# Hyena's filter inputs loaded first, both filters' taps with places of their own, and the second response behind the first modulation rows

## The chip, the cores and the metric

One core of a Trainium2 chip runs the whole program in one launch. The metric is the time of one execution on the device in microseconds (us), as a median over several runs.

## The reference, cut to what matters

Two transformer blocks (DEPTH = 2) work on a context of 256 tokens and a latent of 256 tokens, width 1024. Every block has a modulated FFN (SwiGLU, hidden width 2816), a mixer, and a second FFN. The first block's mixer holds a Hyena segment. What the change touches are the inputs of these steps:

```python
m_lat = jnp.split(s_lat @ ada_w[l] + ada_b[l], 9, axis=-1)        # modulation, s = silu(c)
h_lat = post_norm_residual(h_lat, swiglu(modulate(h_lat, m_lat[0], m_lat[1]), ...), ...)
...
def hyena_filters(L, w1, b1, f1, w2, b2, f2, w3):
    h = jnp.sin(f1 * (z @ w1 + b1))       # z: (L, 33), constant
    h = jnp.sin(f2 * (h @ w2 + b2))       # (L, 64)
    h = (h @ w3).astype(f32).reshape(L, HY_ORDER, 2, HY_W)         # 2 filters, 2 directions, 512 channels
    return h * window[:, None, None, :]
```

The filters depend on parameters alone. Each filter's two directions are combined and taken to the frequency domain by products with a matrix of cosines and sines. The kernel calls that its response, and it is used only in the Hyena segment, far behind the first FFN.

## The kernel before, in words

The tokens stand feature by feature in eight tiles `h[:, k]` of 128 features and 512 tokens (256 of context, 256 of latent). Products with large weights are made three times in a rounded format: ScalarE copies a piece of weights or a tile of tokens to its rounded value (`hi`, L629, and `u_round`, L666), GpSimd or VectorE forms the remainder (L2033, L1552), and TensorE adds hi*hi, hi*lo and lo*hi. A gate/up pair of the first FFN is 2 times 8 times 3 = 48 such products of 512 columns. Products of full fp32 operands (`mm`, L948) appear in the profile as two passes each.

Every engine has one fixed order of work, and engines wait for each other on semaphores. SP issues the loads of large weights on its queue; ScalarE issues all the others on its own queue before its first computation. The arena in SBUF is one buffer whose ranges are used again by stages that follow one another.

The start of the program, up to the first FFN, is what the change reorders:

- Loads. SP: six blocks of modulation weights (`load_ada`, L458, 1.5 MB each, blocks c = 0 to 5), then, once three of them are used, chunk 0 of the up/gate weights (L467), blocks 6 and 7, and chunk 1. ScalarE's queue (L564): identity, 18 parameter rows, four token tiles of 512 KB, the 12 filter inputs under semaphore `ld_filt` (zT, w1, w2, four columns of hyp with 64 elements each, w3, window, skip, dft, sin0), and four constants. w3, window, dft and sin0 are 1.66 MB together.
- TensorE: parameter rows turned (L953), tokens turned in eight banks of PSUM (L960) and copied by ScalarE (L614); then w1's product, modulation blocks 0 and 1, w2's product, blocks 2 to 4, the taps of filter 0 (`taps_of`), block 5, the response of filter 0 (`response_of`, 10 products of fp32, 20 passes), block 6, the taps of filter 1, block 7, the turn of the modulation rows (`ada_turn`), the response of filter 1, and a wait for its copies.
- VectorE: after w1's and w2's product the argument of the sine in seven steps (L1491 to L1502), then for each filter the window product (L1532), two corrections of one row, difference and sum (L1537, L1539). Both filters use the same SBUF ranges `taps` and `tap_m`, and the same banks of PSUM, so `taps_free` (raised in VectorE's code) holds back filter 1's taps until filter 0's response is computed and copied. `modulation(0)` (L1509 to L1521) follows both filters.
- ScalarE: Silu of c, token copies, two Sin, copies of response 0 (`filter_out`, L640 and L642), copy of the modulation rows (L619), copies of response 1, four weight pieces (`first_pieces`, L629), then for each k the modulated tile and its rounded copy (`u_round(0)`, L661 and L666).
- The first gate/up pair (`first_pair`) needs these tiles one by one. SP waits for both responses (`filt_dft` 2) before it loads the second row of modulation weights and chunk 2 of up/gate.

## Time and profile before

| | |
|---|---|
| median of 3 runs | 2609.51 us (2609.12 to 2609.9) |
| profiled execution, its own time | 2611.09 us |
| its span | 2609.3 us |
| mean granted TensorE clock | 0.921 |
| TensorE busy | 2260.9 us, 87% |
| VectorE, ScalarE, GpSimd busy | 971.6, 743.0, 932.6 us |

The span is the stretch from the first to the last instruction in one profiled execution; the own time is what that execution took on the device. Engines work beside each other, so their shares do not add up. An idle stretch matters only where it lies on the chain of waits that ends last. PE is TensorE, PEld its weight load, DVE VectorE, ACT ScalarE, POOL GpSimd, SPq and ACTq the queues on which SP and ScalarE issue loads.

### The profile page before, as it was taken

How to read it: one execution, taken by the hardware profiler on the slowest of the kernel's cores; microseconds unless marked ns; L12 is line 12 of the kernel's file. 1: busy time of each engine (PE TensorE's matmuls, PEld its weight loads, DVE VectorE, ACT ScalarE, POOL GpSimd, SP SyncE). 2: the span in 40 equal slices, each digit the busy share in tenths (PEclk: the TensorE clock that was granted, in tenths of full speed). 3: DMA queues.
4: the chain of work that ended last, by engine and by line, in shares of the span. 5: the costliest groups of instructions: out<-in, count | busy, mean ns of one | idle time of the engine just before them, and what ended most of it. 6: DMA issues, size and time to landing. Idle time of an engine off the chain costs nothing.

```text
span 2609.3 us, 35528 instructions
## 1 busy us (share of the span) xinstructions
PE 2260.9 (87%) x15423; PEld 1833.2 (70%) x15423; DVE 971.6 (37%) x1412; ACT 743.0 (28%) x1080; POOL 932.6 (36%) x421
## 2 busy tenths in 40 slices
PE   5799999899956687786899999799999898468996
PEld 2477877588435687685677877577888687367996
DVE  2333032522486545545533022532133400635312
ACT  1412121443031111013622122432122354115433
POOL 0244434354042101102443434343444353015884
PEclk8799999899987898888999999899999898658998
DMA  9164354131000000002264354255222130013551
GB/s 329 57 208 143 121 174 153 65 115 55 12 1 2 2 3 2 2 3 97 89 201 145 121 178 154 89 169 194 95 94 87 41 135 33 0 65 107 192 186 65
DMA packets 176091, 259.66 MB, mean 100 GB/s; under 512 B 3925, under 2 KB 146275, under 8 KB 175876
## 3 DMA queue, kind: packets, MB, share of 16 engines
q1 hardware_dynamic: 172192, 250.62, 28.7%
q10 hardware_dynamic: 3748, 6.81, 0.8%
q8 instruction: 121, 1.98, 0.3%
q14 instruction: 30, 0.25, 0.0%
HBM read 256.37 MB, written 1.05 MB: 99 GB/s over the span
## 4 chain that ended last, share of the span: by engine, by line
PE 77%; DVE 14%; ACT 5%; issue 2%; DMA 1%; ACTq 1%; POOL 0%; DVEq 0%; POOLq 0%
PE psum L948 76%; DVE arena L1819 2%; ACT arena L661 2%; ACT u_hi L666 1%; DVE arena L1793 1%; DVE arena L1843 1%; DVE h L1603 1%; DMA arena<-k_sin 1%; ACTq L564 1%; DVE arena L1760 1%; DVE arena L1841 0%; DVE arena L1771 0%; DVE tmp L1616 0%; ACT tmp L711 0%; DVE arena L1737 0%
## 5 line engine op out<-in xcount | busy, mean ns | idle before, releaser
L2033 POOL TENSOR_TENSOR w_lo<-arena,w_hi 128x1024 fp32r<-128x1024 f32 x332 | 813.0, 2454 | 1162.9 <-ACT w_hi L629 1160.4
L948 PE MATMUL psum<-u_hi,w_hi 128*128 128x512 f32 (+1 forms) x1888 | 700.3, 371 | 84.9 <-ACT u_hi L666 49.5
L948 PE MATMUL psum<-u_hi,w_lo 128*128 128x512 f32 (+1 forms) x1888 | 689.1, 365 | 0.0
L948 PE MATMUL psum<-u_lo,w_hi 128*128 128x512 f32 (+1 forms) x1888 | 668.7, 362 | 0.0
L629 ACT ACTIVATE w_hi<-arena 128x1024 fp32r<-128x1024 f32 x332 | 348.4, 1056 | 746.2 <-PE psum L948 734.5
L948 PE MATMUL psum<-arena 64*64 64x64 f32 (+7 forms) x5828 | 440.1, 276 | 104.0 <-DVEq L1799 27.7
L948 PEld LDWEIGHTS psum<-u_hi,w_hi 128*128 128x128 f32 x1888 | 362.7, 192 | 184.4 <-issue 50.1
L948 PEld LDWEIGHTS psum<-arena 64*64 64x64 f32 (+4 forms) x5828 | 356.5, 165 | 181.3 <-issue 70.5
L948 PEld LDWEIGHTS psum<-u_hi,w_lo 128*128 128x128 f32 x1888 | 363.2, 192 | 54.1
L948 PEld LDWEIGHTS psum<-u_lo,w_hi 128*128 128x128 f32 x1888 | 357.5, 190 | 52.8 <-issue 0.2
L1573 DVE TENSOR_TENSOR tmp<-psum,tmp 128x512 f32<-128x512 f32 (+1 forms) x88 | 54.9, 624 | 593.0 <-ACT tmp L685 593.0
L948 PE MATMUL psum<-hid_hi,w_hi 128*128 128x512 f32 (+1 forms) x704 | 257.4, 366 | 1.7 <-POOL w_lo L2033 1.2
L948 PE MATMUL psum<-hid_hi,w_lo 128*128 128x512 f32 (+1 forms) x704 | 255.3, 363 | 0.0
L948 PE MATMUL psum<-hid_lo,w_hi 128*128 128x512 f32 (+1 forms) x704 | 255.2, 363 | 0.0
L1577 DVE TENSOR_TENSOR hid_lo<-tmp,hid_hi 128x512 f32 (+1 forms) x88 | 198.7, 2258 | 10.8
L948 PEld LDWEIGHTS psum<-hid_hi,w_hi 128*128 128x128 f32 x704 | 132.9, 189 | 24.5 <-DVE mods L1509 1.7
L948 PEld LDWEIGHTS psum<-hid_lo,w_hi 128*128 128x128 f32 x704 | 132.9, 189 | 21.1 <-issue 0.7
L948 PEld LDWEIGHTS psum<-hid_hi,w_lo 128*128 128x128 f32 x704 | 132.9, 189 | 20.7
L685 ACT ACTIVATE tmp<-psum 128x512 f32<-128x512 f32 (+1 forms) x88 | 47.9, 544 | 303.3 <-PE psum L948 303.2
L815 ACT ACTIVATE arena<-psum 128x256 f32<-128x256 f32 x96 | 37.1, 386 | 239.3 <-PE psum L948 238.7
L1587 DVE SCALAR_TENSOR_TENSOR h<-psum,mods,h 128x256 f32<-128x256 f32 x56 | 22.3, 475 | 197.3 <-PE psum L948 197.3
L1603 DVE SCALAR_TENSOR_TENSOR h<-psum,mods,h 128x256 f32<-128x256 f32 x80 | 35.2, 478 | 147.9 <-PE psum L948 147.9
(245 smaller groups left out, 1637.9 us busy)
## 6 DMA issues: line engine op xcount, KB each, us to landing
arena<-in_ada_w SPq DMA_DIRECT2D x48, 1536.0 KB, 7.0
arena<-in_ffn_wg SPq DMA_DIRECT2D x44, 1024.0 KB, 5.4
arena<-in_ffn_wu SPq DMA_DIRECT2D x44, 1024.0 KB, 8.0
arena<-in_ffn_wd SPq DMA_DIRECT2D x20, 2048.0 KB, 8.0
arena<-in_ev_w_in SPq DMA_DIRECT2D x6, 2048.0 KB, 7.8
arena<-in_od_w_in SPq DMA_DIRECT2D x6, 2048.0 KB, 8.3
arena<-in_ffn_wd SPq DMA_DIRECT2D x4, 1024.0 KB, 5.0
arena<-in_ev_w_out SPq DMA_DIRECT2D x2, 2048.0 KB, 10.8
```

Of the source, the lines that this page charges most:

```text
L564: act.dma_start(dst, src).then_inc(S(name), 16)
L629: act.activation(piece_shape(split_hi(pc), src), src, ACT.Copy).then_inc(S("hi_done"), 1)
L661: ins = act.activation(us[:, k, s_], hs[:, k, s_], ACT.Identity, scale=modv[:, 24 * (g % 3) + 8 + k, s_:s_ + 1], bias=modv[:, 24 * (g % 3) ...
L666: act.activation(uhv[:, k, T0:NT], uv[:, k, T0:NT], ACT.Copy).then_inc(S("u_hi"), 1)
L685: act.activation(tmp[:, jf * NT:jf * NT + TN], bank[2 * jf][:, 0:TN], ACT.Silu)\
L815: act.activation(blocks(zs[:, d].rearrange("p h t -> p (h t)"), m, d), blocks(bank[d], m, d), ACT.Copy).then_inc(S("zs"), 1)
L948: return pe.matmul(dst, w, x, start=first_, stop=last, skip_group_check=True)
L1573: ve.tensor_tensor(prod, bank[2 * jf + 1][:, 0:TN], prod, ALU.mult).then_inc(S("pairs_free"), 1)
L1577: ve.tensor_tensor(hid_lo[:, at], prod, hid_hi[:, at].bitcast(F32), ALU.subtract)\
L1603: ins = ve.scalar_tensor_tensor(out=hs[:, k, s], in0=bank[b][:, lo:lo + SEG], scalar=modv[:, 24 * (g % 3) + 16 + k, s:s + 1], in1=hs[:, k, s],
L1819: ve.copy_predicated(nm[:, d, 2 * cc + e].rearrange("p (q a) t -> p q (a t)", q=2), mk, bank[n_bank(d, cc, e)].rearrange("p (q t) -> p q t ...
L2033: pool.tensor_tensor(piece_shape(split_lo(pc), src), src, piece_shape(split_hi(pc).bitcast(F32), src), ALU.subtract).then_inc(S("lo_done"), 1)
```

## The change

The seven inputs of the filter's MLP are issued first on SP's queue under a semaphore of their own (`ld_mlp`), modulation block 0 follows, then the five large or late filter inputs (`ld_filt`), then blocks 1 to 5. The MLP's two products stand ahead of and between the parameter rows' and the tokens' turns; the sine's argument is a function that VectorE calls ahead of and behind the parameter copies, and ScalarE's Sin, Silu, Sin stand ahead of the token copies. Tokens are turned in a ring of five banks. The taps of each filter have SBUF ranges of their own, so that only the PSUM banks are waited for (`taps_read`); the two responses use different banks for two of their five results. dft and sin0 lie in a part of the arena that modulation block 0 has not got. TensorE computes the taps of both filters and the first response between the blocks 0 to 3, then blocks 4 to 7 and their turn, then the second response. Its copies on ScalarE follow `u_round(0)`, and the wait for them stands ahead of the second gate/up pair. The first weight pieces stand ahead of the modulation rows' copy.

```diff
@@ -260,6 +260,8 @@
+        TOK_RING = 5
+
@@ -274,8 +276,9 @@
         stage = [big[:, 4096 + i * P:4096 + (i + 1) * P] for i in range(3)]
         w3 = big[0:HY_FO, 4608:6656]
         win = big[:, 6656:7680].rearrange("p (a c) -> p a c", a=2)
-        taps = big[:, 7680:9728].rearrange("p (d a c) -> p d a c", d=2, a=2)
-        tap_m = big[:, 9728:10752].rearrange("p (a c) -> p a c", a=2)
+        taps = [at.rearrange("p (d a c) -> p d a c", d=2, a=2) for at in (big[:, 7680:9728], big[:, 2048:4096])]
+        tap_m = [at.rearrange("p (a c) -> p a c", a=2) for at in (big[:, 9728:10752], big[:, 4608:5632])]
+        FILT_BANK = ((0, 1, 3, 4, 5), (6, 7, 3, 4, 5))
@@ -287,8 +290,8 @@
         kf = arena[:, 40448:45568].rearrange("p (o i c) -> p o i c", o=2, i=5)
-        dft = arena[:, 16384:17408].rearrange("p (a f) -> p a f", a=2)
-        sin0 = arena[:, 18432:18688].rearrange("p (a f) -> p a f", a=2)
+        dft = arena[:, 44544:45568].rearrange("p (a f) -> p a f", a=2)
+        sin0 = arena[:, 43520:43776].rearrange("p (a f) -> p a f", a=2)
@@ -530,7 +533,21 @@
-            for c in range(6):
+            def load_filter(name, dst, src):
+                sp.dma_start(dst, src).then_inc(S(name), 16)
+
+            load_filter("ld_mlp", zT, K["k_zT"])
+            load_filter("ld_mlp", fw1, A["hy_f_w1"][0])
+            for i, name in enumerate(("hy_f_b1", "hy_f_freq1", "hy_f_b2", "hy_f_freq2")):
+                load_filter("ld_mlp", hyp[0:HY_FO, i:i + 1], A[name].rearrange("e n -> n e"))
+            load_filter("ld_mlp", fw2, A["hy_f_w2"][0])
+            load_ada(0, 0)
+            load_filter("ld_filt", w3, A["hy_f_w3"][0])
+            load_filter("ld_filt", big[:, 6656:7680], K["k_win"])
+            load_filter("ld_filt", skip_row, A["hy_skip"].rearrange("e o c -> e o c"))
+            load_filter("ld_filt", arena[:, 44544:45568], K["k_dft"])
+            load_filter("ld_filt", arena[:, 43520:43776], K["k_sin0"])
+            for c in range(1, 6):
                 load_ada(0, c)
             sp.wait_ge(S("ada_used"), 3)
             load_up("up_a", 0, 0, 0)
@@ -590,28 +607,22 @@
             for b in range(4):
                 src = A["ctx"] if b < 2 else A["x"]
                 load("ld_tok", tok_in[:, b, :], src[0, (b % 2) * P:(b % 2 + 1) * P, :])
-            load("ld_filt", zT, K["k_zT"])
-            load("ld_filt", fw1, A["hy_f_w1"][0])
-            load("ld_filt", fw2, A["hy_f_w2"][0])
-            for i, name in enumerate(("hy_f_b1", "hy_f_freq1", "hy_f_b2", "hy_f_freq2")):
-                load("ld_filt", hyp[0:HY_FO, i:i + 1], A[name].rearrange("e n -> n e"))
-            load("ld_filt", w3, A["hy_f_w3"][0])
-            load("ld_filt", big[:, 6656:7680], K["k_win"])
-            load("ld_filt", skip_row, A["hy_skip"].rearrange("e o c -> e o c"))
-            load("ld_filt", arena[:, 16384:17408], K["k_dft"])
-            load("ld_filt", arena[:, 18432:18688], K["k_sin0"])
             load("ld_const", mean_w[:, :], K["k_mean"])
             load("ld_const", blk[:, :], K["k_blk"])
             load("ld_const", ones[:, :], K["k_ones"])
             load("ld_const", masks[:, :], K["k_masks"])
 
 
+            act.wait_ge(S("sin_arg"), 1)
+            act.activation(h1, pre, ACT.Sin).then_inc(S("sin_done"), 1)
             act.wait_ge(S("par_done"), 1)
             act.activation(sgc[:, :], par[:, PAR["c"]:PAR["c"] + 16], ACT.Silu).then_inc(S("silu_c"), 1)
+            act.wait_ge(S("sin_arg"), 2)
+            act.activation(h2, pre, ACT.Sin).then_inc(S("sin_done"), 1)
 
             for k in range(KT):
                 act.wait_ge(S("tok_turned"), k + 1)
-                act.activation(hv[:, k], bank[(k + 1) % 8], ACT.Copy).then_inc(S("h_ready"), 1)
+                act.activation(hv[:, k], bank[1 + k % TOK_RING], ACT.Copy).then_inc(S("h_ready"), 1)
 
             def ada_out(g):
 
@@ -636,19 +647,15 @@
 
             def filter_out(o):
                 act.wait_ge(S("filt_dft"), o + 1)
-                for i, b in ((0, 0), (1, 1), (2, 3), (3, 4), (4, 0)):
-                    act.activation(kf[:, o, i], bank[b], ACT.Copy).then_inc(S("kf_done"), 1)
+                b = FILT_BANK[o]
+                for i, at in ((2, 2), (3, 3), (0, 0), (1, 1), (4, 0)):
+                    act.activation(kf[:, o, i], bank[b[at]], ACT.Copy).then_inc(S("kf_done"), 1)
                 act.wait_ge(S("kf_done"), 6 * o + 5)
-                act.activation(kf[0:1, o, 4], bank[5][0:1], ACT.Copy).then_inc(S("kf_done"), 1)
-
-            act.wait_ge(S("sin_arg"), 1)
-            act.activation(h1, pre, ACT.Sin).then_inc(S("sin_done"), 1)
-            act.wait_ge(S("sin_arg"), 2)
-            act.activation(h2, pre, ACT.Sin).then_inc(S("sin_done"), 1)
+                act.activation(kf[0:1, o, 4], bank[b[4]][0:1], ACT.Copy).then_inc(S("kf_done"), 1)
+
             filter_out(0)
+            first_pieces(0, 0, PIECES)
             ada_out(0)
-            filter_out(1)
-            first_pieces(0, 0, PIECES)
 
             def u_round(g):
 
@@ -925,6 +932,8 @@
 
             for g in range(SUBS):
                 u_round(g)
+                if g == 0:
+                    filter_out(1)
                 if g:
                     first_pieces(g, 2, PIECES)
                     h_affine(g - 1)
@@ -947,17 +956,21 @@
             def mm(dst, w, x, first_, last):
                 return pe.matmul(dst, w, x, start=first_, stop=last, skip_group_check=True)
 
+            pe.wait_ge(S("ld_mlp"), 16 * 7)
+            mm(bank[6][0:HY_FO, 0:SEG], fw1, zT, True, True).then_inc(S("filt_mm"), 1)
             pe.wait_ge(S("ld_ident"), 16)
             pe.wait_ge(S("ld_par"), 16 * 18)
             for i, n in enumerate((120, 120, 125)):
                 ins = pe.transpose(bank[0][:, i * P:i * P + n], stage[i][0:n, :], ident[0:n, 0:n])
             ins.then_inc(S("par_turned"), 1)
+            pe.wait_ge(S("sin_done"), 1)
+            mm(bank[7][0:HY_FO, 0:SEG], fw2, h1, True, True).then_inc(S("filt_mm"), 1)
             pe.wait_ge(S("ld_tok"), 64)
             for k in range(KT):
-                if k == KT - 1:
-                    pe.wait_ge(S("par_done"), 1)
+                if k >= TOK_RING:
+                    pe.wait_ge(S("h_ready"), k - TOK_RING + 1)
                 for b in range(4):
-                    ins = pe.transpose(bank[(k + 1) % 8][:, b * P:(b + 1) * P], tok_in[:, b, k * P:(k + 1) * P],
+                    ins = pe.transpose(bank[1 + k % TOK_RING][:, b * P:(b + 1) * P], tok_in[:, b, k * P:(k + 1) * P],
                                        ident[:, :])
                 ins.then_inc(S("tok_turned"), 1)
 
@@ -1004,7 +1017,8 @@
                 ins.then_inc(S("ada_used"), 1)
 
             def taps_of(o):
-                pe.wait_ge(S("taps_free"), o + 1)
+                if o:
+                    pe.wait_ge(S("taps_read"), o)
                 for dr in range(2):
                     for a in range(2):
                         ins = mm(bank[4 + 2 * dr + a], h2[:, a * P:(a + 1) * P],
@@ -1013,38 +1027,34 @@
 
             def response_of(o):
                 pe.wait_ge(S("taps"), o + 1)
+                pe.wait_ge(S("taps_read"), 2)
                 if o:
                     pe.wait_ge(S("kf_done"), 6 * o)
+                b = [bank[i] for i in FILT_BANK[o]]
                 for a in range(2):
                     st, en = a == 0, a == 1
...
-                    ins = mm(bank[5][0:1], dft[:, a, 2 * P:2 * P + 1], taps[:, 0, a], st, en)
+                    mm(b[0], dft[:, a, 0:P], taps[o][:, 0, a], st, en)
+                    mm(b[1], dft[:, a, P:2 * P], taps[o][:, 0, a], st, en)
+                    mm(b[2], sin0[:, a], tap_m[o][:, a], st, en)
+                    mm(b[3], dft[:, a, 3 * P:4 * P], tap_m[o][:, a], st, en)
+                    ins = mm(b[4][0:1], dft[:, a, 2 * P:2 * P + 1], taps[o][:, 0, a], st, en)
                 ins.then_inc(S("filt_dft"), 1)
 
             pe.wait_ge(S("h_ready"), KT)
-            pe.wait_ge(S("ld_filt"), 16 * 12)
-            mm(bank[6][0:HY_FO, 0:SEG], fw1, zT, True, True).then_inc(S("filt_mm"), 1)
+            pe.wait_ge(S("sin_done"), 2)
+            pe.wait_ge(S("ld_filt"), 16 * 5)
+            taps_of(0)
             pe.wait_ge(S("sc_ready"), 1)
             ada(0, 0)
             ada(0, 1)
-            pe.wait_ge(S("sin_done"), 1)
-            mm(bank[7][0:HY_FO, 0:SEG], fw2, h1, True, True).then_inc(S("filt_mm"), 1)
             ada(0, 2)
+            taps_of(1)
             ada(0, 3)
-            ada(0, 4)
-            pe.wait_ge(S("sin_done"), 2)
-            taps_of(0)
-            ada(0, 5)
             response_of(0)
-            ada(0, 6)
-            taps_of(1)
-            ada(0, 7)
+            for c in range(4, AN):
+                ada(0, c)
             ada_turn(0)
             response_of(1)
-            pe.wait_ge(S("kf_done"), 12)
 
             def ffn(g):
                 f = FFN.index(g)
@@ -1058,6 +1068,8 @@
                             pe.wait_ge(S("y_part"), KT * f + 2 * q + 2)
                         if t == 0:
                             first_pair(g, up, [bank[a][:, 0:TN] for a in range(2)], slice(T0, NT), ("gate_mm", "gu_ready"))
+                        if g == 0 and t == 1:
+                            pe.wait_ge(S("kf_done"), 12)
                         for a in range(2) if t else ():
                             pc = piece0[up, g] + 2 * q + a
                             pe.wait_ge(S("lo_done"), pc + 1)
@@ -1447,6 +1459,26 @@
             for i, val in enumerate((LN_EPS / ALPHA ** 2, GLA_EPS, GN_EPS, 1.0)):
                 ve.memset(eps[:, i:i + 1], val).then_inc(S("ve_steps"), v.step())
             ve.wait_ge(S("ve_steps"), v.n)
+
+            def sine_argument(i):
+
+                ve.wait_ge(S("filt_mm"), i + 1)
+                if i:
+                    ve.wait_ge(S("sin_done"), 1)
+                ve.tensor_scalar(pre, bank[6 + i][0:HY_FO, 0:SEG], hyp[0:HY_FO, 2 * i:2 * i + 1],
+                                 hyp[0:HY_FO, 2 * i + 1:2 * i + 2], ALU.add, ALU.mult).then_inc(S("ve_steps"), v.step())
+                ve.wait_ge(S("ve_steps"), v.n)
+                ve.tensor_scalar(turns, pre, 1 / TWO_PI, MAGIC, ALU.mult, ALU.add).then_inc(S("ve_steps"), v.step())
+                ve.wait_ge(S("ve_steps"), v.n)
+                ve.tensor_scalar(turns, turns, MAGIC, None, ALU.subtract).then_inc(S("ve_steps"), v.step())
+                ve.wait_ge(S("ve_steps"), v.n)
+                for part in (PI_A, PI_B, PI_C):
+                    ve.scalar_tensor_tensor(out=pre, in0=turns, scalar=-part, in1=pre, op0=ALU.mult,
+                                            op1=ALU.add).then_inc(S("ve_steps"), v.step())
+                    ve.wait_ge(S("ve_steps"), v.n)
+                ve.tensor_scalar(pre, pre, 3.1415925, -3.1415925, ALU.min, ALU.max).then_inc(S("sin_arg"), 1)
+
+            sine_argument(0)
             ve.wait_ge(S("par_turned"), 1)
             for i, n in enumerate((120, 120, 125)):
                 ve.tensor_copy(par[:, i * P:i * P + n], bank[0][:, i * P:i * P + n]).then_inc(S("ve_steps"), v.step())
@@ -1467,7 +1499,6 @@
             ve.sem_inc(S("par_done"), 1)
             ve.sem_inc(S("pairs_free"), 1)
             ve.sem_inc(S("pairs_free"), 1)
-            ve.wait_ge(S("silu_c"), 1)
             ve.wait_ge(S("ld_ident"), 16)
             ve.tensor_reduce(sel[:, :], ident[:, :].rearrange("p (j m) -> p m j", m=32)[:, 0:2 * AN, :],
                              mybir.AxisListType.X, ALU.add).then_inc(S("ve_steps"), v.step())
@@ -1475,6 +1506,7 @@
             def pad_silu():
 
                 sc2 = scp.rearrange("p (k m) -> p k m", m=SPAN)
+                ve.wait_ge(S("silu_c"), 1)
                 ve.memset(scp, 0.0).then_inc(S("ve_steps"), v.step())
                 ve.wait_ge(S("ve_steps"), v.n)
                 ve.tensor_copy(sc2[:, :, 2 * AN - 1], sgc[:, 0:8]).then_inc(S("ve_steps"), v.step())
@@ -1482,24 +1514,8 @@
                 ve.wait_ge(S("ve_steps"), v.n)
                 ve.sem_inc(S("sc_ready"), 1)
 
+            sine_argument(1)
             pad_silu()
-
-            for i in range(2):
-                ve.wait_ge(S("filt_mm"), i + 1)
-                if i:
-                    ve.wait_ge(S("sin_done"), 1)
...
-                ve.tensor_scalar(pre, pre, 3.1415925, -3.1415925, ALU.min, ALU.max).then_inc(S("sin_arg"), 1)
 
             def modulation(g):
 
@@ -1524,23 +1540,21 @@
                 ve.wait_ge(S("ve_steps"), v.n)
                 ve.sem_inc(S("mods"), 1)
 
-            ve.sem_inc(S("taps_free"), 1)
             for o in range(2):
                 ve.wait_ge(S("filt_taps"), o + 1)
                 for dr in range(2):
                     for a in range(2):
-                        ve.tensor_tensor(taps[:, dr, a], bank[4 + 2 * dr + a], win[:, a], ALU.mult).then_inc(S("ve_steps"), v.step())
-                ve.wait_ge(S("ve_steps"), v.n)
-                ve.memset(taps[0:1, 1, 0], 0.0).then_inc(S("ve_steps"), v.step())
-                ve.tensor_tensor(taps[0:1, 0, 0], taps[0:1, 0, 0], skip_row[:, o], ALU.add).then_inc(S("ve_steps"), v.step())
-                ve.wait_ge(S("ve_steps"), v.n)
-                ve.tensor_tensor(tap_m, taps[:, 0], taps[:, 1], ALU.subtract).then_inc(S("ve_steps"), v.step())
-                ve.wait_ge(S("ve_steps"), v.n)
-                ve.tensor_tensor(taps[:, 0], taps[:, 0], taps[:, 1], ALU.add).then_inc(S("taps"), 1)
-                if o == 0:
-                    ve.wait_ge(S("filt_dft"), 1)
-                    ve.wait_ge(S("kf_done"), 6)
-                    ve.sem_inc(S("taps_free"), 1)
+                        ve.tensor_tensor(taps[o][:, dr, a], bank[4 + 2 * dr + a], win[:, a], ALU.mult)\
+                            .then_inc(S("ve_steps"), v.step())
+                ve.wait_ge(S("ve_steps"), v.n)
+                ve.sem_inc(S("taps_read"), 1)
+                ve.memset(taps[o][0:1, 1, 0], 0.0).then_inc(S("ve_steps"), v.step())
+                ve.tensor_tensor(taps[o][0:1, 0, 0], taps[o][0:1, 0, 0], skip_row[:, o], ALU.add)\
+                    .then_inc(S("ve_steps"), v.step())
+                ve.wait_ge(S("ve_steps"), v.n)
+                ve.tensor_tensor(tap_m[o], taps[o][:, 0], taps[o][:, 1], ALU.subtract).then_inc(S("ve_steps"), v.step())
+                ve.wait_ge(S("ve_steps"), v.n)
+                ve.tensor_tensor(taps[o][:, 0], taps[o][:, 0], taps[o][:, 1], ALU.add).then_inc(S("taps"), 1)
 
             modulation(0)
             ve.wait_ge(S("ld_const"), 64)
```

## Rows read from the trace of the kernel before

**Rows 1.** The page: TensorE's share of the span, and its granted clock by slices.
```profile
PE 2260.9 (87%) x15423; PEld 1833.2 (70%) x15423; DVE 971.6 (37%) x1412; ACT 743.0 (28%) x1080; POOL 932.6 (36%) x421
...
PEclk8799999899987898888999999899999898658998
```

**Rows 2.** Chain of waits by time, 16 to 125 us: start, us, what.
```profile
16.58 15.83 DMA arena<-k_sin
...
53.03 11.95 PE psum L948 x25
...
68.27 6.77 PE psum L948 x8
...
75.06 2.50 DVE arena L1532 x4
...
81.31 11.46 PE psum L948 x20
...
95.88 3.88 ACT w_hi L629 x4
...
112.98 12.08 PE psum L948 x52
```

**Rows 3.** Windows: length, busy of PE, PEld, DVE, ACT, POOL, clock, DMA share, GB/s.
```profile
2.00:4.00 2.00, 0.00 (x0) 0.00 (x0) 0.00 (x0) 0.00 (x0) 0.00 (x0) 1.00 0.92 196
...
20.00:30.00 10.00, 5.39 (x32) 5.15 (x32) 0.87 (x4) 5.08 (x10) 0.00 (x0) 1.00 1.05 298
...
38.00:40.00 2.00, 2.00 (x22) 0.60 (x18) 0.82 (x2) 0.00 (x0) 0.00 (x0) 0.99 1.06 372
...
62.00:64.00 2.00, 2.00 (x9) 0.63 (x11) 0.00 (x0) 0.00 (x0) 0.00 (x0) 1.00 0.57 180
...
68.00:70.00 2.00, 1.73 (x3) 0.93 (x4) 0.00 (x0) 0.17 (x1) 0.00 (x0) 0.69 0.00 0
```

**Rows 4.** Modulation loads L458: SP's six, block 0's landing, block 7's issue and landing.
```profile
0.74 29.70 SPq L458 DMA_DIRECT2D arena<-in_ada_w  x6
...
DMA to landing us min/median/max: 8.0/8.0/8.0
...
L458 SPq DMA_DIRECT2D arena<-in_ada_w x1: 3360/3360/3360, 43.6 to 43.6; - x1
...
DMA to landing us min/median/max: 14.6/14.6/14.6
```

**Rows 5.** Timeline, 10 to 108 us: start, us, engine, line, operation, idle before.
```profile
10.60 0.40 ACTq L564 DMA_DIRECT2D arena<-k_zT  x1
...
13.93 0.62 ACTq L564 DMA_DIRECT2D hyp<-in_hy_f_freq  x1
...
19.23 1.28 ACT L610 ACT_TABLE_LOAD   x1 [19.23 <-issue]
...
20.89 5.39 PE L960 MATMUL psum<-ident,arena 128*128 128x128 f32 x32 [6.79 <-DMA arena<-in_x]
...
24.57 2.56 ACT L614 ACTIVATE h<-psum 128x512 f32<-128x512 f32 x5 [0.22 <-PE psum L960]
...
33.55 4.98 PE L948 MATMUL psum<-arena,rs 128*32 128x384 f32 x32
...
36.55 0.42 ACT L645 ACTIVATE arena<-arena 64x256 f32<-64x256 f32 x1 [9.42 <-DVE arena L1502]
...
39.03 4.08 PE L948 MATMUL psum<-arena,rs 128*32 128x384 f32 x48
...
43.04 3.70 PE L948 MATMUL psum<-arena 64*128 64x512 f32 x8
...
78.35 1.46 PE L948 MATMUL psum<-sel,arena 128*128 128x16 f32 x6 [0.61 <-ACT arena L619]
...
107.42 0.37 SPq L467 DMA_DIRECT2D arena<-in_ffn_wg  x1
```

**Rows 6.** Window behind the first gate/up pair, columns as in rows 3.
```profile
117.00:160.00 43.00, 43.00 (x209) 33.51 (x208) 15.38 (x12) 10.18 (x13) 19.70 (x8) 1.00 0.39 125
```

12 lines of the change are left out of this document (removed).

## The prediction

> **What bounds the kernel now.** I read the page first, then the chain of waits in order of time, then the windows for granted clock and DMA rate, and last the timeline of the first 120 us. The page says that TensorE is busy 87% of the span, but its granted clock has two low slices, 8 and 7 tenths, at the very start, in the first 130 us [rows 1]: the change's stage is one of the loose ones. The chain shows why [rows 2]: it runs through the landing of k_sin0 (32.4), PE, VectorE making the first filter's taps, the first response (53.03 to 65), the second filter's tap product only from 68.27, VectorE again (75.06 to 81.31), the second response (81.31 to 92.8), ScalarE's copies, then 3.88 us of weight pieces on ScalarE, and then the eight modulated tiles until 112.98. Of the 52 products that follow in 12.08 us, 0.232 us each, the first 20 are the rest of the first gate/up pair, which so ends at 117.6. From there PE is busy 43.00 of 43 us at clock 1.00 [rows 6]. So whatever moves the end of the first pair moves the end of the program one for one, as long as nothing behind it is late. I call this time M; M is 117.6 before.
>
> While this goes on, DMA has its own bound: the stream of modulation and FFN weights runs near 370 GB/s from 4 us until 63 [rows 3]. The last modulation block, c=7, was issued at 43.6 and landed 14.6 us later, at 58.2 [rows 4]; PE took it up at 74.95. The wait for it is the floor of any reordering here.
>
> **Part 1, the loads.** Seven small loads (zT, w1, four columns of hyp, w2) go to the head of SP's queue. The same seven took ScalarE's queue from 10.60 to 14.55 to issue, 0.62 us for a column [rows 5]: 4.0 us by which the first modulation block, issued at 0.74 before [rows 4], is late. The stream is full afterwards, so the last block is late too. Something comes back. In 20 to 30 us the engines were full but moved 298 GB/s, and at 2 to 4 us 196, against 372 in 38 to 40 [rows 3]; I put that down to small packets (at the start the parameters, later the hyp columns of four bytes), which now fall in the idle gap. The deficits are 10 x 74/372 = 2.0 us and 1 us. Bounds of the shift: 1.0 and 4.0 us. I take 1.5, nearer the low one since both deficits are seen: block 7 lands at 59.7. The big filter loads (1.66 MB with w3, window, dft, sin0) now follow block 0 on SP's queue: block 0 landed 8.0 us after its issue at 0.74 [rows 4], now at 12.8; then 1.7 MB at half of 372 GB/s, beside the tokens on ScalarE's queue, is 9.4 us: 22.2. They are wanted at 27.1, spare 5 us. The Trainium skill (DMA: Bandwidth & Descriptors, "Anatomy of one DMA", written for GpSimd's path) gives a transfer about 2 us of fixed cost and speaks so against tiny loads at a queue's head: one after another the seven would take 14 us, an estimate from that page, and by it the sum would be 10 us worse. The trace speaks against adding them up: k_sin0 was the 35th load of its queue and had landed at 32.4 with all ahead of it [rows 2], under 1 us for each with the big ones among them.
>
> **Part 2, the MLP ahead of the tokens.** The small loads are there by about 7. From the landing at 32.41 [rows 2] to the end of Sin at 36.97 [rows 5] a layer took 4.6 us, twice over some 9 us. ScalarE is free of its issues at about 12.8 (19.23 less the twelve loads from 10.60 to 17.0) [rows 2, 5], so Sin, Silu, Sin run between 12.8 and 20. The tokens are turned from 20.89 [rows 5], copied until 27.1. All of this is covered; without cover it would be 9 us. One rule speaks against it. The trace shows one table load of 1.28 us for Silu and none before Sin at 36.55 [rows 5], so that one table served both; with Sin first another table may be picked. Two more loads are 2.6 us, ending near 20.8, still ahead of the first copy at 22. The Trainium skill (ScalarE: Activation LUTs, "Rules for kernel authors") budgets 2.7 us for each switch of set; three would be 8 us by that page instead of my 3.8, and could push the copies by some 4 us. The ring of five banks instead of eight makes turn k wait for copy k-5, which is always done, since a copy follows its turn by one: nothing.
>
> **Part 3, both taps early.** From 27.1 on PE has no load to wait for: taps 3.70 for eight passes, three blocks of modulation 4.08 (48 passes), taps again 3.70 [rows 5], so 38.6. VectorE's 6.25 us for the first taps lie under that (30.8 to 37.1); its four products of the second, 2.5 us [rows 2], end at 41.1 and release the first response. That takes at most the 11.5 us of before: 52.6. Blocks 4, 5, 6 are 4.1: 56.7. PE then waits 3.0 us for block 7. Removed is the handover in which the second taps waited for the first filter's copies (65.0 to 68.27), then PE 6.77 and VectorE 6.25.
>
> **Part 4, modulation before the second response.** Block 7 at 59.7 runs after an idle stretch; such stretches ended in a granted clock of 0.5 before (0.69 on the mean of 68 to 70) [rows 3], the 1.2 GHz level. At that level 32 passes took 4.98 [rows 5], so 16 take 2.5: 62.2. Row copy 0.5, turn 1.46 [rows 5]: 64.2. Then the second response on PE, 11.46 with half of it at the low level as before [rows 2]: 75.7. Beside it VectorE finishes mods at 64.6 and ScalarE modulates eight tiles in 13.2 us (99.76 to 112.98) [rows 2]: 77.8. The first pair starts on PE at 75.7, directly behind dense work, at the full level: 48 products at 12.08/52 = 0.232 us [rows 2] are 11.1 us, so **M = 86.8**. The last tile is wanted at 75.7 + 6.5 = 82.2 and is there at 77.8. Moved off the chain: the first weight pieces (3.88) run at about 55.3 to 59.2, while PE waits for block 7; GpSimd's 10.3 us behind them end near 67. The second filter's copies (3.15) run 77.8 to 80.9, and the new wait ahead of the second pair (kf_done 12) is met 6 us early. Behind that wait stand only that pair's products. SP waits for the second response before the next block and chunk 2 of the up weights, now at 75.7 for a pair that starts at the same time; before, chunk 2 was issued at 107.42, 10 us before M [rows 5], so it is 11 us before M again. The last stage runs as before, since PE was its bound.
>
> **Sum.** 117.6 - 86.8 = 30.8 us. The profiled execution's span is 2609.3 in a run of 2611.09; that becomes 2578.5 and 2580.3. The runs' median, 2609.51, is 0.2 above the span, so I forecast **2578.7**.
>
> **Bounds.** Stream shift 1.0 to 4.0: M from 86.3 to 89.3. Second response wholly at the full level (20 x 3.70/8 = 9.3): M 84.6, and with block 7 too (1.4) 83.5; ScalarE's tiles then allow no less than 77.8 + 1.0 + 3.8 = 82.6. All PE work from 27.1 to 41 at the low level (taps 6.77 each, blocks 7.5) adds 9.6: block 7 ends at 67.7 instead, but then PE has had no idle stretch, the response takes 9.3: M about 90. Likeliest case 2574 to 2583.
>
> **Rivals.** (a) The stream of weights is the bound and later than I think: its head is held by the small loads or by the filter's 1.7 MB. Each us late at block 7 is a us at M. For it: PE has only 3.0 us of spare ahead of block 7. Against it: total bytes are the same. 5 to 10 us late gives 2583.5 to 2588.5. (b) Better: both clock gains and an early stream, M about 80, if PE reaches full level and mods come at 59: 2572. Against it: the idle stretch before block 7. (c) No change: TensorE stays at 1.2 GHz all the way. From 27.1: 6.8 + 7.5 + 6.8 + 2.5, response 16.9, four blocks 10, turn 2, response 16.9, pair 48 x 0.46 = 22: M about 117.5, 2609.4. Against it: the full level came back within 38 to 40 (0.99) [rows 3] after six us of such work, though not during the taps at 68 to 75, whose eight passes took 6.77 us instead of 3.70 [rows 2, 5]. (d) Slower: ScalarE now stands at the wait for the first sine argument ahead of Silu and of all token copies. If the seven loads landed at L, the copies start at L + 9; that is free up to L = 13, with 3 us more of spare ahead of block 7, so from L = 16 + 31 = 47 on it is slower than before, and L = 60 gives 2622. Small loads at the head of an empty queue against block 0's 1.5 MB, landed in 8.0 us, leave it hardly a chance. (e) The gain is given back in the FFN, because chunks or GpSimd bind there: 10 to 20 us kept, 2590 to 2600. Against it: PE without an idle us behind M [rows 6].
>
> **Chances.** My forecast (2574 to 2583.5) 0.76, (a) 0.12, (b) 0.06, (e) 0.02, (c) 0.02, (d) 0.02. The range 2571 to 2588 leaves out little more than (c), (d), (e) and the tail of (a). A measurement of this kernel tells 0.2% (5 us) from no change: faster 0.96, same 0.02, slower 0.02.
>
> **What would show it.** Right: the first sine argument before the token turns; taps of filter two ending near 39; one idle stretch of PE of some 3 us ahead of block 7, and block 7 landing at 59 to 61; mods at 64 to 65; no PE gap between second response and first pair; M at 84 to 90, and everything behind it shifted by one amount. Wrong: block 7 after 65, clock 0.5 through both responses, or a PE gap before the second pair or behind chunk 2.

## The result and the profile after

The changed kernel took 2580.88 us in the median of four runs (2579.05 to 2581.12), the kernel before 2609.61 (2609.12 to 2609.9): 28.7 us less, a ratio of 0.9889 with a 95% interval of 0.9871 to 0.9906. The forecast was 2578.7 in a range of 2571 to 2588. The profiled execution took 2581.12 with a span of 2579.3, which is 30.0 below the span of before.

The page of the changed kernel: TensorE's share and its granted clock by slices, which answer to [rows 1].

```profile
PE 2251.7 (87%) x15423; PEld 1832.2 (71%) x15423; DVE 969.1 (38%) x1412; ACT 744.3 (29%) x1081; POOL 931.8 (36%) x421
...
PEclk9999999899969987898999999899999898658998
```

The two first slices read 9 and 9 instead of 8 and 7. The twelfth and thirteenth read 6 and 9 where they read 8 and 7 before. For the most part that is one stretch of some 60 us that both kernels have, from about 640 us behind the first silu on, in which PE is mostly idle and the clock low: it lies some 30 us earlier now, more in the twelfth slice and less in the thirteenth. What the even mixer loses is smaller, and comes below.

The chain of waits of the changed kernel by time, the counterpart of [rows 2].

```profile
11.35 12.69 DMA arena<-in_x
...
30.71 7.75 PE psum L957 x56
...
42.19 4.53 SPq L461
...
46.77 14.18 DMA arena<-in_ada_w
...
60.99 1.54 PE psum L957 x16
...
62.56 0.50 ACT arena L630
...
63.10 46.95 PE psum L957 x197
```

VectorE's taps, ScalarE's response copies, its weight pieces and its modulated tiles have all left the chain. In their place stands one landing, that of modulation block 7 at 60.95. From 63.10 on PE alone carries the chain, as far as this view goes (110).

The timeline of the changed kernel, the counterpart of [rows 5].

```profile
7.46 0.54 DVE L1468 TENSOR_SCALAR arena<-psum,hyp 64x256 f32<-64x256 f32 x1 [6.51 <-PE psum L957]
...
13.77 1.28 ACT L617 ACT_TABLE_LOAD   x1 [13.77 <-issue]
...
15.49 1.28 ACT L619 ACT_TABLE_LOAD   x1
...
22.18 0.42 ACT L621 ACTIVATE arena<-arena 64x256 f32<-64x256 f32 x1 [3.08 <-DVE arena L1479]
...
44.77 8.77 PE L957 MATMUL psum<-arena 128*128 128x512 f32 x19 [1.29 <-DVEq L1550]
...
58.28 9.30 POOL L2047 TENSOR_TENSOR w_lo<-arena,w_hi 128x1024 fp32r<-128x1024 f32 x4 [57.83 <-ACT w_hi L640]
...
60.99 1.50 PE L957 MATMUL psum<-arena,rs 128*32 128x384 f32 x16 [2.73 <-DMA arena<-in_ada_w]
...
63.79 9.21 PE L957 MATMUL psum<-arena 128*128 128x512 f32 x20
...
64.22 1.07 DVE L1537 SCALAR_TENSOR_TENSOR mods<-mods,eps 128x16 f32<-128x16 f32 x1
...
78.58 2.53 ACT L652 ACTIVATE arena<-psum 128x512 f32<-128x512 f32 x5
...
84.14 0.60 ACT L692 ACTIVATE tmp<-psum 128x512 f32<-128x512 f32 x1 [0.69 <-PE psum L957]
```

The last row is the first silu of the FFN. It starts when the first gate/up pair is finished and marks M well. In the kernel before it is this row of the same view:

```profile
117.84 0.60 ACT L685 ACTIVATE tmp<-psum 128x512 f32<-128x512 f32 x1 [0.69 <-PE psum L948]
```

So the first pair ends 33.70 us earlier. The windows of the changed kernel, columns as in [rows 3], show the DMA gap at the start, a second dip of DMA at 12 to 14 us, the clock around block 7, and the FFN behind the first pair, which is as dense as in [rows 6].

```profile
2.00:4.00 2.00, 0.00 (x0) 0.00 (x0) 0.00 (x0) 0.00 (x0) 0.00 (x0) 1.00 0.33 84
4.00:6.00 2.00, 0.00 (x0) 0.00 (x0) 0.00 (x0) 0.00 (x0) 0.00 (x0) 1.00 0.23 42
...
12.00:14.00 2.00, 0.00 (x0) 0.00 (x0) 0.00 (x0) 0.23 (x1) 0.00 (x0) 1.00 0.92 192
...
60.00:62.00 2.00, 1.01 (x15) 0.42 (x16) 0.00 (x0) 0.97 (x2) 2.00 (x2) 1.00 1.09 348
...
84.14:127.14 43.00, 43.00 (x208) 33.52 (x207) 15.38 (x12) 10.42 (x12) 19.48 (x9) 1.00 0.43 141
```

**Where 33.7 became 30.0.** I followed ScalarE's table loads, which stand at the same places of both programs. Counted from the first silu, the load ahead of the even mixer's tanh starts at 553.1 us in both. The next two start at 630.8 and 637.3 before, but at 632.4 and 640.5 after, so 3.3 us are lost between 553 and 641. From there to the last one the distance changes by 0.6. The windows of that stretch, of the changed kernel:

```profile
700.14:702.14 2.00, 2.00 (x6) 0.74 (x5) 1.71 (x5) 0.69 (x1) 0.00 (x0) 0.67 0.00 0
702.14:704.14 2.00, 2.00 (x7) 1.29 (x7) 1.89 (x7) 0.78 (x2) 0.00 (x0) 0.50 0.00 0
...
716.14:718.14 2.00, 1.44 (x3) 0.68 (x4) 1.82 (x4) 1.97 (x3) 0.10 (x1) 0.93 0.00 0
718.14:720.14 2.00, 2.00 (x4) 0.87 (x3) 2.00 (x2) 0.92 (x2) 2.00 (x1) 0.50 0.00 0
```

and of the kernel before, where the same work lies 33.7 us later:

```profile
732.00:736.00 4.00, 2.62 (x9) 1.45 (x10) 3.60 (x8) 1.25 (x2) 0.00 (x0) 1.00 0.00 0
736.00:740.00 4.00, 4.00 (x20) 2.40 (x18) 4.00 (x14) 3.66 (x7) 0.00 (x0) 1.00 0.00 0
...
748.00:752.00 4.00, 3.19 (x8) 1.55 (x9) 3.82 (x6) 3.48 (x5) 0.85 (x1) 1.00 0.00 0
```

The same instructions ran at the 1.2 GHz level after and at 2.4 GHz before, behind stretches in which PE waits for VectorE and works only in part (0.62 of 2.00 us at 698.14 to 700.14, 1.44 at 716.14 to 718.14). Whether the change causes that or it is a draw is one question of the experiments.

### The profile page after: what moved, and what is told of

Read it like the earlier page. It is cut to its first block, busy times and chain, and to the rows that moved or that the text cites. A ratio compares the mean times of both kernels' runs of the same rounds, so it can differ in the third digit from the quotient of the medians.

```text
span 2579.3 us, 35529 instructions
## 1 busy us (share of the span) xinstructions
PE 2251.7 (87%) x15423; PEld 1832.2 (71%) x15423; DVE 969.1 (38%) x1412; ACT 744.3 (29%) x1081; POOL 931.8 (36%) x421
## 4 chain that ended last, share of the span: by engine, by line
PE 77%; DVE 14%; ACT 4%; issue 2%; DMA 1%; ACTq 0%; SPq 0%; POOL 0%; DVEq 0%; POOLq 0%
PE psum L957 77%; DVE arena L1833 2%; ACT arena L668 1%; ACT u_hi L673 1%; DVE arena L1807 1%; DVE arena L1857 1%; DVE h L1617 1%; DMA arena<-in_ada_w 1%; DVE arena L1774 1%; DVE arena L1855 1%; DVE arena L1785 1%; DMA arena<-in_x 0%; DVE tmp L1630 0%; ACT tmp L718 0%; ACTq L581 0%
```

## The experiments

The other question is which part carries the gain. For each kernel I read the first silu (M) and the rest, from the first silu to the last table load. The runs, in the order of this section:

| kernel | first silu | rest | median | ratio to before (95%) |
|---|---|---|---|---|
| before | 117.84 | 2473.4 | 2609.61 | |
| changed | 84.14 | 2477.3 | 2580.88 | 0.9889 (0.9871 to 0.9906) |
| changed, again | 87.39 | 2474.0 | 2580.90 | 0.9881 (0.9864 to 0.9897) |
| changed, third | 85.65 | 2473.9 | 2579.95 | 0.9882 (0.9865 to 0.9898) |
| two idle products | 85.99 | 2472.9 | 2580.61 | 0.9885 (0.9868 to 0.9901) |
| four idle products | 87.70 | 2471.4 | 2582.95 | 0.9894 (0.9878 to 0.9911) |
| response ahead of the turn | 96.70 | 2472.8 | 2589.22 | 0.9912 (0.9896 to 0.9929) |
| turn first, in the kernel before | 109.51 | 2474.1 | 2603.09 | 0.9972 (0.9961 to 0.9982) |
| one home for the taps | 89.38 | 2473.9 | 2584.17 | 0.9897 (0.9881 to 0.9913) |
| loads on ScalarE's queue | 93.83 | 2471.4 | 2584.67 | 0.9897 (0.9881 to 0.9914) |
| block 0 first | 81.45 | 2472.9 | 2574.91 | 0.9864 (0.9847 to 0.9880) |
| block 0 first, again | 81.46 | 2472.7 | 2575.23 | 0.9866 (0.9850 to 0.9883) |
| block 0 first, pieces split | 81.62 | 2472.1 | 2574.76 | 0.9864 (0.9848 to 0.9881) |

The two middle columns are of one profiled execution each. The medians are of four runs, eight for the turn first. The kernels were timed in four groups, each beside the kernel before: the changed kernel alone; the changed kernel again with the response ahead, one home and ScalarE's queue; the two with idle products with the turn first and block 0 first; and the changed kernel a third time with block 0 first again and the split pieces. The kernel before read 2609.61, 2611.87, 2610.77 and 2610.59 in them, so a difference of 1 or 2 us between groups says little.

### The changed kernel again

No edit.

> The changed kernel once more, nothing edited. In its first profile the first silu stands 33.7 us earlier than before (84.14 against 117.84), the span only 30.0 us; 3.3 us went in the even mixer, where the granted clock was 0.57 in one window of 4 us that stood at 1.00 before. If the clock's drop there is fixed by where the kernel's work falls in time, it is seen again and the time is 2580 to 2581. If it is chance from run to run, some runs are near 2577.

Measured: the lost stretch of the even mixer was there again in the profile (third table load at 640.6 from the first silu), and the time was 2580.90. But the first silu stood at 87.39 instead of 84.14, with the same loads and the same work, and the distance behind the mixer was shorter by 3.3. The windows of this run, PE alone (busy, granted clock, DMA share, GB/s):

```profile
62.00:64.00 2.00, 1.41 (x14) 0.60 1.09 347
64.00:66.00 2.00, 2.00 (x7) 0.50 0.60 189
```

Block 7 arrived at 61.2, PE had waited for it for 2.73 us, and this time the clock fell to its 1.2 GHz level at 62.4 and stayed there until near 69. In the first profile the same wait left it at 1.00. So neither place is fixed by the kernel.

> The changed kernel a third time, beside the two variants below on the same chip: the span is the first silu's time plus a rest that has read 2471.4 to 2477.3 us from the first silu to the last table load, whatever the kernel. First silu 84 to 87.5, median 2579 to 2582.

Measured: first silu 85.65, rest 2473.9, median 2579.95, as expected. The clock fell at 60.6, in the wait itself, and was back at 64. In the mixer the third table load stood at 637.2, as in the kernel before: the loss of 3.3 us was not there.

### Idle products ahead of the first pair

```diff
+                        if g == 0 and t == 0:
+                            for _ in range(2):      # 4 in the other kernel
+                                mm(bank[0], ident[:, :], hv[:, 0], True, True)
                         if t == 0:
                             first_pair(g, up, ...)
```

> The changed kernel with 2 idle fp32 products (identity times a token tile, result overwritten) ahead of the first pair on PE: everything behind is 1.85 us later. If the loss of 3.3 us in the even mixer depends on where that work falls against the clock's windows, it can vanish: then the total is 1.4 us below the changed kernel's (2579.5) with clock 1.00 in the window that had 0.57. If the loss belongs to what the change computes or to its place in memory, it stays, and the total is 1.85 us above (2582.7).

> As delay2 with 4 products, 3.7 us later (8 passes at 0.46). Windows of the clock: the loss of 3.3 us may vanish, then the total is 0.4 us above the changed kernel (2581.3). Loss fixed to the change: 3.7 us above (2584.6).

Measured: the first silu moved by 1.85 and 3.56 us, as the products cost. In both profiles the rest was shorter, 2472.9 and 2471.4 against 2477.3, and the spans were 2576.7 and 2576.9, below the undelayed 2579.3. With two products the drop behind the mixer's second wait was gone and the first stayed; with four both were gone. But each of these profiles is of the fastest of four runs: the other three took 2580.57 to 2581.01 and 2582.63 to 2583.76. The medians, 2580.61 and 2582.95, lie between what the two theories gave (2579.5 or 2582.7, and 2581.3 or 2584.6), and neither kernel was timed beside the changed one, so they do not decide.

What decides the first half of the question is the third profile of the changed kernel, and those of the kernels below that compute the same: the loss does not belong to what the change computes or to its place in memory, since the unedited kernel was without it once. Whether it follows from the place in time stays open. The three profiles of the changed kernel reach the mixer at three different times (first silu 84.14, 87.39 and 85.65), so they do not speak against it; nor were they all taken on one chip. For whoever compares two kernels it acts as a draw: over the three profiles of the changed kernel the rest varies by 3.4 us, over the 13 profiles of the table by 6.0.

### The second response ahead of blocks 6, 7 and the turn

```diff
             response_of(0)
-            for c in range(4, AN):
-                ada(0, c)
-            ada_turn(0)
+            ada(0, 4)
+            ada(0, 5)
             response_of(1)
+            ada(0, 6)
+            ada(0, 7)
+            ada_turn(0)
```

with `filter_out(1)` back behind `filter_out(0)`.

> The changed kernel with the second response (and its copies) put ahead of blocks 6 and 7 and the turn; all else as changed. Theory (moving the turn ahead of the second response is the main gain): PE does response 1 at about 57 to 66.5, blocks 6, 7 and turn end near 71, mods 72, ScalarE's eight tiles then bound the first pair: first silu about 92 to 94 instead of 84.1, total 8 to 10 us above the changed kernel, 2589 to 2591. Rival (the early loads and the taps' homes are the main gain, the place of the response counts for little): within 3 us of the changed kernel.

Measured: 2589.22, 8.3 us above the changed kernel and inside the expectation; the first silu at 96.70 is 2.7 later than its upper end. The chain of this kernel:

```profile
57.90 9.21 PE psum L956 x25
...
67.14 2.56 ACT arena L652 x5
...
70.22 3.88 ACT w_hi L640 x4
...
74.09 0.38 ACT arena L630
...
91.81 28.47 PE psum L956 x133
```

The rows' copy at 74.09 queues on ScalarE behind the response's copies and the weight pieces (70.22 to 74.09); I had left those pieces out, and the mods' last step was stretched as well (76.26 to 78.40). The eight tiles then end at 91.8, as ScalarE's part of the chain did before. The place of the second response is worth about 8 us, the largest of the three parts that were taken out of the changed kernel singly.

### The turn first, in the kernel before

Loads, MLP and the shared home stay as before; dft and sin0 lie at the changed kernel's place, and response 1 uses banks 6 and 7.

```diff
             ada(0, 6)
-            taps_of(1)
             ada(0, 7)
             ada_turn(0)
+            taps_of(1)
             response_of(1)
-            pe.wait_ge(S("kf_done"), 12)
...
+                if o:
+                    modulation(0)
                 ve.wait_ge(S("filt_taps"), o + 1)
```

> The kernel before with only the turn put ahead: blocks 6 and 7, the turn and modulation first, then the second taps and response, ScalarE's tiles ahead of the second response's copies, first weight pieces ahead of them; dft and sin0 at the changed kernel's place, loads and MLP as before. Theory: block 7 is taken at 66 instead of 75, mods near 69.5, but PE still does taps (3.7 to 6.8), waits VectorE's 6.2 and does the response (9 to 11.5) ahead of the first pair: first silu 98 to 106 instead of 117.8, 12 to 19 us faster than before. Rival (the late MLP and taps bound it, the order of the turn hides nothing): under 5 us faster.

Measured: 2603.09, 7.7 us faster than the kernel before beside it (2610.77), between the theory's 12 to 19 and the rival's under 5, so neither had it; the first silu, 109.51, is 3.5 us later than the theory's upper end. The chain:

```profile
71.60 8.60 PE psum L949 x14
...
80.22 2.50 DVE arena L1536 x4
...
86.48 33.65 PE psum L949 x115
```

The turn and the second taps take 8.60 us together, VectorE 6.26, and the response begins at 86.48 with the granted clock at 0.50 from 72 to near 92. The modulated tiles are hidden, as meant, but the second filter's taps now stand between the turn and the response, at half clock. The order alone gives a quarter of the gain. By this chain it needs the taps done beforehand.

### One home for both filters' taps

```diff
-        taps = [... for at in (big[:, 7680:9728], big[:, 2048:4096])]
+        taps = [... for at in (big[:, 7680:9728], big[:, 7680:9728])]
...
             ada(0, 2)
-            taps_of(1)
             ada(0, 3)
             response_of(0)
+            ada(0, 4)
+            ada(0, 5)
+            taps_of(1)            # behind kf_done 6
```

with `tap_m` shared as well.

> The changed kernel with one SBUF home for both filters' taps again: the second taps wait for the first response's copies and stand between block 5 and block 6. Theory (the landing of block 7, 61.0, is the floor, and the second taps fit ahead of it): PE's taps 53.5 to 57.5, VectorE until 63.7, block 7 at 61 to 62.5, response 1 at 64: first silu within 1 us of 84.1, total within 1 us of the changed kernel. Rival (the homes carry the gain, since the handover of the taps was on the chain before): 6 to 12 us slower, as VectorE's 6.2 us and PE's 3.7 us come back onto the chain.

Measured: 2584.17, 3.3 us above the changed kernel, first silu 89.38. Neither theory had the size. The timeline shows what I had not priced:

```profile
55.16 9.77 POOL L2048 TENSOR_TENSOR w_lo<-arena,w_hi 128x1024 fp32r<-128x1024 f32 x4 [54.71 <-ACT w_hi L640]
...
61.02 1.69 DVE L1553 TENSOR_TENSOR arena<-arena 1x512 f32<-1x512 f32 x1
...
62.75 3.25 DVE L1556 TENSOR_TENSOR arena<-arena 128x1024 f32<-128x1024 f32 x1
...
67.32 3.45 PE L957 MATMUL psum<-arena 128*128 128x512 f32 x4 [3.44 <-DVE arena L1558]
```

The difference of the taps took 3.25 us where it takes 1.23 elsewhere, and the one-row sum 1.69 instead of 0.62, both while GpSimd formed the weight pieces' remainders. The sum of the taps behind them (66.04, with GpSimd idle) took its usual 1.23. Without the two long steps VectorE would have finished at 64.2, an estimate from 61.02 with 0.62, 1.23 and 1.24, and the theory (response at 64) would have held. The rest of the delay is the clock, at 0.50 from 67.7 to 71. The homes are worth some 3 us here, and by this timeline they are so because they move the second taps' VectorE work to a time when GpSimd is idle.

### The filter's loads back on ScalarE's queue

```diff
-            load_filter("ld_mlp", zT, K["k_zT"])
...
             load_ada(0, 0)
-            load_filter("ld_filt", w3, A["hy_f_w3"][0])
...
+            load("ld_mlp", zT, K["k_zT"])          # ScalarE, behind the tokens
...
+            load("ld_filt", w3, A["hy_f_w3"][0])
```

> The changed kernel with all twelve filter loads back on ScalarE's queue behind the tokens; order of the work as changed. Theory (a late MLP delays PE by some 8 us, of which 3 us are spare ahead of block 7, and block 7 lands 2 to 3 us earlier): sine arguments behind the tokens' landing, tokens copied by about 37 to 39 instead of 30.7, first silu 87 to 90, total 3 to 6 us above the changed kernel. Rival (the title's first part carries the gain): 15 us or more slower. Rival 2 (the loads first cost more than they bring): faster than the changed kernel.

Measured: 2584.67, 3.8 us above the changed kernel, inside 3 to 6. The timeline:

```profile
24.02 1.11 PE L957 MATMUL psum<-arena 33*64 33x256 f32 x2 [24.02 <-DMA hyp<-in_hy_f_freq]
...
37.09 3.74 PE L957 MATMUL psum<-arena 64*128 64x512 f32 x6 [1.75 <-ACT h L625]
```

The first taps begin at 37.09 instead of 30.71. The first silu, 93.83, lies 4 to 7 us later than I expected, because the clock was at 0.50 from 39 to 45.7 and from 73 to 76.4; the rest, 2471.4, happened to be the shortest of the table, as with four idle products. The median is the better measure: loads first are worth about 4 us, not 15, and they do not cost more than they bring.

Taken out singly, the three parts cost 8.3, 3.3 and 3.8 us, 15.4 together, of a gain of some 30. The other half belongs to no part singly: each of these kernels keeps the two other parts, and the order of the turn without them gained 7.7 in the kernel before.

### Modulation block 0 ahead of the seven small loads

```diff
+            load_ada(0, 0)
             load_filter("ld_mlp", zT, K["k_zT"])
...
             load_filter("ld_mlp", fw2, A["hy_f_w2"][0])
-            load_ada(0, 0)
```

> The changed kernel with modulation block 0 issued ahead of the seven small loads. Theory: DMA ran at 10 to 84 GB/s until 6 us in the changed kernel; with block 0 at the head the stream starts 4 us sooner, block 7 lands at 57 to 58 instead of 61.0, PE's 2.7 us of idle ahead of it goes, and the small loads (landing about 10) are still hidden: first silu 81 to 82 instead of 84.1, total 2 to 3 us faster if the clock behind does the same. Rival: the small loads behind 1.5 MB land so late that the sine chain delays the tokens: slower by 1 to 4 us.

> Modulation block 0 ahead of the seven small loads again, timed in five rounds beside the changed kernel. Theory: first silu at 81.5 again, 2.7 us ahead of the best of the changed kernel, so the median is 2 to 6 us lower (2575 to 2578). Rival (the first reading was only luck with the clock behind the start): equal medians.

Measured: first silu at 81.45 and 81.46, medians 2574.91 and 2575.23. The changed kernel timed beside the second of them took 2579.95: 4.7 us more. The DMA gap at 2 to 6 us is closed, and a dip has moved to 6 to 12 us, as the windows of the first show:

```profile
2.00:4.00 2.00, 0.00 (x0) 0.00 (x0) 0.00 (x0) 0.00 (x0) 0.00 (x0) 1.00 0.95 236
4.00:6.00 2.00, 0.00 (x0) 0.00 (x0) 0.00 (x0) 0.00 (x0) 0.00 (x0) 1.00 1.07 393
...
8.00:10.00 2.00, 0.00 (x0) 0.00 (x0) 0.00 (x0) 0.00 (x0) 0.00 (x0) 1.00 0.85 192
10.00:12.00 2.00, 0.36 (x1) 0.28 (x2) 0.00 (x0) 0.00 (x0) 0.00 (x0) 1.00 0.86 203
```

Block 7 landed at 58.1 to 58.4 us instead of 60.95 to 61.2, and against the profile of the changed kernel in which the clock did not fall the first silu is 2.7 us earlier. The other 2 us fit the clock: in none of the three profiles of this order (with the one below) did it fall ahead of the first silu, while it did in two of five with the changed order, those with idle products included. With so few profiles that may be chance. PE's wait ahead of block 7 was 1.3 to 1.5 us here and 2.7 in all five there; that the shorter wait is the cause was not tested by itself.

### The same with the weight pieces split

```diff
             filter_out(0)
-            first_pieces(0, 0, PIECES)
+            first_pieces(0, 0, 2)
             ada_out(0)
+            first_pieces(0, 2, PIECES)
```

> The same with two of the four first weight pieces behind the modulation rows' copy instead of ahead of it. There the chain ran ScalarE's 3.88 us of pieces (56.02 to 59.90) into the rows' copy, while block 7 was used near 58.4. Theory: the copy at 58.4, everything behind 1.0 to 1.5 us earlier, first silu about 80; ScalarE's tiles then end near 76 and just feed the first pair. Rival: the pieces only move into the tiles' way and nothing is won, or the pair waits for the tiles: first silu 81.5 to 83.

Measured: 2574.76, first silu 81.62; nothing is won. The chain of the unsplit kernel, then that of the split one:

```profile
56.11 3.88 ACT w_hi L640 x4
...
59.99 0.38 ACT arena L630
```

```profile
44.20 14.18 DMA arena<-in_ada_w
...
58.43 1.54 PE psum L958 x16
```

The pieces did leave the chain. What is behind them is block 7 again, landing at 58.38: two bounds lay within 0.1 us of each other. But from 2 us until then DMA moved 353 GB/s on the mean, against some 373 from 26 to 42 us; the dip at 6 to 12 us is 2.3 us of the stream, an estimate from 296, 192 and 203 GB/s in its three windows against 373. So a further gain at the start has to fill that dip or load fewer bytes ahead of block 7, and neither was tried. These two orders, with the pieces split or not, are the best of the study, equal within what the runs tell.

## Why the prediction was right, by its own steps

**The mechanism.** M moved from the chain of taps, response and tiles to block 7's landing, and the gain passed on one for one through the FFN. M was forecast at 86.8; the first silu minus 0.24 (its distance to M before) gives 83.9, 87.2 and 85.4 in the three profiles. The gain at M was 33.7, 30.5 and 32.2 against 30.8. The chain shows the mechanism, and the experiment with block 0 ahead bears it out, where the landing and the first silu moved together by 2.7 us.

**Part 1, sizes off in both directions.** Block 7 landed at 60.95, not 59.7. The gap of DMA cost more than I gave back: the shift was 2.8, inside its bounds of 1.0 to 4.0, and I took 1.5. I had put the 298 GB/s of 20 to 30 us down to small packets and expected most of that back. About half came, 1 of 2 us as an estimate from the windows: the columns landed ahead of 6.24, and yet DMA moved only 192 GB/s at 12 to 14. What passes there, from 11.0 to 13.7 by the packets' records, are the 64 rows of 8 KB of w3, and before they passed from 22.1 to 26.2, in the two lowest windows of that stretch (216 and 227 GB/s). The small loads did overlap: the seven issued in 4.0 us had landed when PE started at 6.24, so the 14 us that the forecast worked out from the Trainium skill (DMA: Bandwidth & Descriptors, "Anatomy of one DMA") for loads one after another did not appear. What I missed is the tokens: they landed at 24.04 instead of near 20.9. ScalarE's queue issued them at 10.01 instead of 8.77; rows ahead of them that took 0.32 to 0.48 us to issue before took 0.59 to 0.64 beside SP's small loads. The other 1.9 us went in the transfers, beside block 0 and the large filter inputs. The parameters had landed at 16.5 instead of 13.3. The first taps began at 30.71 instead of 27.1.

**Part 2** held. The sine argument began at 7.46, the second Sin ended at 22.6, ahead of the tokens. The trace has two table loads, one for Sin and one for Silu, and none for the second Sin: 1.28 us more than before, hidden under waiting. Neither my third load nor the 2.7 us of the Trainium skill (ScalarE: Activation LUTs, "Rules for kernel authors") was seen; a load is 1.28 us in this trace.

**Part 3** had two errors that in part cancelled. It began 3.6 us late, and the first response took 9.2 us instead of at most 11.5, with the clock at 1.00 throughout. PE's idle stretch ahead of block 7 was 2.73 us for a forecast 3.0.

**Part 4** had the clock term too large, 3.95 us: I charged 1.1 on block 7, 0.6 on the turn and 2.25 on the response. The first profile had none of it (block 1.50, turn 0.84, response 9.21), the second 3.0 (1.72, 1.46, 11.37), the third 1.3, all on block 7 (2.79, 0.84, 9.21). The first is the case of my bounds in which response and block 7 run wholly at the full level, 83.5 there and 83.9 measured. The new wait for kf_done 12 was met at 81.7, 2 us early, not 6. The tiles ended at 78.7 for a last need at 79.5: the cover was 0.8 us, not 4.4, since the modulation's last step took 1.07 instead of 0.17 beside GpSimd and PE was ahead. I had left GpSimd's work on the first weight pieces (58.28 to 67.58) out of account for VectorE.

**"The last stage runs as before"** is the step that failed. As work it is the same, but from the first silu on it took 3.9 us more in the first profile, of which 3.3 are the clock in the even mixer. In the two other profiles of the same kernel it took 0.5 to 0.6 more than before. In spans, M was 2.9 us better than forecast and the rest 3.9 worse, which leaves about 1 (2579.3 against 2578.5). That these two errors cancel is luck; at M the forecast was off by 2.9, 0.4 and 1.4 us in the three profiles. The other 1.4 of the 2.2 us between 2580.88 and 2578.7 lie in the medians: that of before is 1.5 below the profiled execution's own time, that of the changed kernel 0.2. Two sums of the forecast are off and bear on nothing: rival (c)'s terms give M 118.5, not 117.5, and 1.7 MB at half of 372 GB/s are 9.1 us, not 9.4.

**The rivals.** (a), a late weight stream, described the direction of block 7's error, with 1.3 us instead of 5 to 10. Of (b) the first profile had the clock half, the full level behind block 7, but not the early stream. (c), (d) and (e) did not come: the clock stood at 1.00 up to block 7, no FFN bound appeared (PE is busy 43.00 of 43 us behind the first silu), and ScalarE's wait for the first sine argument, met at 10.3, was over before its issues.

## What to carry to other kernels

When a chain of small stages stands in front of a dense phase, ask which load the last of them needs, and put everything that does not need it in front of that landing: here the second taps and first response, while the second response hides ScalarE's tiles. Then look at the queue's head: seven small loads of 4 us issue time in front of a 60 us stream cost 2.6 us at its end, and putting one large load ahead of them gained more than splitting the weight pieces did. A forecast that ends at the last changed instruction still has to carry the spread of what follows; here that was 3.4 us over three profiles of one kernel and 6.0 over all 13, as large as the errors made at the start.

## What the runs showed of the hardware

- The granted clock around one wait of PE is not settled by the kernel. The same wait of 2.7 us ahead of block 7 left it at 1.00 in three profiles (the first one and the two with idle products, whose code is the same up to there) and let it fall to the 1.2 GHz level in two (back at 64 and near 69). The first silu of the changed kernel varied by 3.25 us, of which 0.3 are a later landing.
- VectorE waits for GpSimd, it is not only slowed. While GpSimd forms w_lo (four steps of 2.35 us each), a step of VectorE with both operands in SBUF did not end before the running step of GpSimd did: the mods' 128x16 step took 1.07, 2.29 and 0.23 us in the three profiles of the changed kernel and ended at 65.30, 67.61 and 65.96, where GpSimd's steps ended at 65.26, 67.57 and 65.92. It takes 0.17 in the kernel before, with GpSimd idle. The step just ahead of it, which reads one operand from PSUM, took 0.21 in all three beside the same work of GpSimd. With one home, two fp32 operands of 128x1024 took 3.25 us instead of 1.23 and ran until 1.1 us behind GpSimd's last end.
- Issues of loads took longer where both queues issued small loads. Single parameter rows took ScalarE's queue 0.59 to 0.64 us beside SP's small loads and 0.32 to 0.48 in the kernel before, and the tokens were issued 1.2 us later. That SP's issues are the cause was not tested by itself.
- DMA dips where the 64 rows of 8 KB of w3 pass: 216 and 227 GB/s at 22 to 26 us before, 192 at 12 to 14 in the changed kernel, 192 and 203 at 8 to 12 with block 0 first, against some 372 in most windows behind. In the changed kernel the filter's small loads had landed before. No run moved w3 alone.
